# A two-block transformer kernel: order of the wide projection's chunks, and the place of the local-attention heads

## What is computed

```python
h = rms_norm(x, norm_mix[i])
u = h @ w_in[i]                                  # 1024 x 8208, row-major float32
(gq, gk, gv, g_lr, g_r, mq, mk, mv, gate_a, gate_b) = jnp.split(u, points, axis=-1)
...
o_a = rms_norm(o_a, gla_out_norm[i]).reshape(B, S, GLA_HEADS * GLA_DV) * jax.nn.silu(g_r)
y_a = o_a @ w_branch_a[i]
qh = rms_norm(mq..., moba_q_norm[i]); kh = rms_norm(mk..., moba_k_norm[i])
y_b = moba_attention(qh, kh, vh) @ w_branch_b[i]   # 8 heads; 256 tokens are one block: causal attention
y = jax.nn.sigmoid(gate_a) * y_a + jax.nn.sigmoid(gate_b) * y_b
x = x + y @ w_out[i]
```

## Time and profile before

| | |
|---|---|
| median of 3 runs | 1248.38 us (1246.42 to 1248.42) |
| profiled execution | 1250.41 us, span 1248.7 us |
| busy: PE, DVE, ACT | 1158.2 us (93%), 772.7 us (62%), 570.5 us (46%) |
| mean granted TensorE clock | 0.964 |

### The profile page before, as it was taken

How to read it: one execution, slowest core, us unless ns; L and a number is a source line. 1 busy time by engine, 2 the same in 40 slices (tenths; PEclk the granted TensorE clock), 3 DMA queues, 4 the chain that set the end, 5 groups by cost and what they waited for, 6 DMA issues and landing times.

```text
span 1248.7 us, 15377 instructions
## 1 busy us (share of the span) xinstructions
PE 1158.2 (93%) x6348; PEld 971.8 (78%) x6348; DVE 772.7 (62%) x868; ACT 570.5 (46%) x783; POOL 62.1 (5%) x118
## 2 busy tenths in 40 slices
PE   4899979899999977699999899999999899999998
PEld 2677756679998756599998687787787788997886
DVE  1586668578878739687554465435656567665444
ACT  2542327565444213354443446654665356545342
POOL 2011120000111100000000000000000000000000
PEclk8999989999999878799999989999999999999999
DMA  9956680157998844387555657878652265655550
GB/s 310 382 193 221 227 292 21 68 183 236 321 339 288 273 165 149 120 266 250 178 184 180 153 122 162 155 151 163 135 200 75 71 219 184 186 183 186 185 177 34
DMA packets 119431, 236.80 MB, mean 190 GB/s; under 512 B 5569, under 2 KB 60162, under 8 KB 119234
## 3 DMA queue, kind: packets, MB, share of 16 engines
q1 hardware_dynamic: 105458, 186.26, 49.8%
q0 software_dynamic: 13904, 49.56, 11.7%
HBM read 234.75 MB, written 1.05 MB: 189 GB/s over the span
## 4 chain that ended last, share of the span: by engine, by line
PE 82%; DVE 6%; DMA 4%; ACT 3%; issue 2%; SPq 2%; DVEq 0%; ACTq 0%
PE ps L1676 17%; PE ps L1677 16%; PE ps L1678 16%; PE ps L1715 7%; PE ps L1714 7%; PE ps L1713 7%; PE ps L1795 2%; DVE modraw L1079 2%; DMA modraw<-in_w_mod 1%; PE ps L1931 1%; PE ps L1944 1%; DMA raw<-in_w_in 1%; DMA mod<-in_w_mod 1%; ACT wH L558 1%; DVE wL L1000 1%
## 5 line engine op out<-in xcount | busy, mean ns | idle before, releaser
L1000 DVE TENSOR_TENSOR wL<-raw,wH 128x1024 fp32r<-128x1024 f32 x328 | 397.6, 1222 | 309.9 <-ACT wH L558 308.5
L558 ACT ACTIVATE wH<-raw 128x1024 fp32r<-128x1024 f32 x328 | 343.1, 1057 | 440.7 <-PE ps L1678 295.9
L1676 PE MATMUL ps<-wH,aH 128*128 128x512 f32 (+1 forms) x624 | 252.6, 405 | 17.8 <-DVE aL L1028 9.9
L1677 PE MATMUL ps<-wL,aH 128*128 128x512 f32 (+1 forms) x624 | 245.8, 394 | 0.0
L1678 PE MATMUL ps<-wH,aL 128*128 128x512 f32 (+1 forms) x624 | 245.3, 393 | 0.0
L1713 PE MATMUL ps<-aH,wH 128*128 128x256 f32 x768 | 219.0, 285 | 0.0
L1715 PE MATMUL ps<-aH,wL 128*128 128x256 f32 x768 | 217.3, 283 | 0.0
L1714 PE MATMUL ps<-aL,wH 128*128 128x256 f32 x768 | 217.3, 283 | 0.0
L1676 PEld LDWEIGHTS ps<-wH,aH 128*128 128x128 f32 x624 | 120.3, 193 | 52.6 <-issue 24.8
L1713 PEld LDWEIGHTS ps<-aH,wH 128*128 128x128 f32 x768 | 147.4, 192 | 0.7 <-issue 0.5
L1714 PEld LDWEIGHTS ps<-aL,wH 128*128 128x128 f32 x768 | 147.4, 192 | 0.7 <-issue 0.7
(11 more groups left out here) (295 smaller groups left out, 1227.2 us busy)
## 6 DMA issues: line engine op xcount, KB each, us to landing
raw<-in_ffn_w_in SPq DMA_DIRECT2D x88, 512.0 KB
modraw<-in_w_mod POOLq DMA_DIRECT2D x80, 512.0 KB, 6.1
raw<-in_w_in SPq DMA_DIRECT2D x32, 1024.0 KB
raw<-in_ffn_w_out SPq DMA_DIRECT2D x22, 1024.0 KB
raw<-in_w_up SPq DMA_DIRECT2D x16, 1024.0 KB
raw<-in_w_down SPq DMA_DIRECT2D x16, 1024.0 KB
mod<-in_w_mod SPq DMA_DIRECT2D x8, 1024.0 KB, 12.5
raw<-in_attn_w_qkv SPq DMA_DIRECT2D x8, 1024.0 KB
```

What stands on the lines that cost most here:

```text
L558: nc.scalar.activation(wH[:, n % WS, :], raw[:, (n // 2) % RAW, (n % 2) * 1024:(n % 2) * 1024 + 1024], ACT.Copy).then_inc(w_hi, 1)
L1000: V.tensor_tensor(wL[:, n % WL, :], raw[:, (n // 2) % RAW, (n % 2) * 1024:(n % 2) * 1024 + 1024], wH[:, n % WS, :].bitcast(fp32), ALU.subt ...
L1676: T.matmul(outp, xh, h, start=first, stop=False)
L1677: T.matmul(outp, xh, l, start=False, stop=False)
```

## The change

The chunks of the projection are taken in the order 0, 2, 1, 3, ... (the loads and the columns of `u` that are written). The `mqk` groups stand behind chunks 12 and 13, four groups each, in banks 4 to 7. Score products 0 and 1, the `oa` groups and `moba(0)` stand inside chunks 14 and 15, `moba(1)` behind chunk 15. `bra` runs tile 0 first, then tile 1, from tiles `oaH` and `oaL` of its own, with the remaining `moba(h)` in front of some of its parts (`hooks`: the pair is sub, tile). The splits of the `brb` weights stand between the heads.

Of the new functions, `mprobs(h)` is the copy of the transposed probabilities that stood in the loop before (it waits for `mtranspose(h)` and for `mvalues(h - 2)`); `gate_a(t)` multiplies tile t of the `bra` product with its gate; `oa_groups(i)` issues groups i and i + 1 of `oa`; `ob_first` waits for all eight `moba_out` and transposes tile 0 of the attention output, `ob_last` tile 1, into banks 6 and 7; `hi_ob` and `lo_ob` write their high and low parts.

```diff
+MQK = (0, 4, 1, 5, 2, 6, 3, 7)
+WIN = (0, 2, 1) + tuple(range(3, 16))
+...
+        def mbank(j):
+            return ps[:, 4 + j % 4, :]
@@ sync queue
-            for c in range(16):
-                chunk(n + 4 * c, a["w_in_2"][0], c * CW if c < 4 else LR0 + GRANK + (c - 4) * CW)
+            for i, c in enumerate(WIN):
+                chunk(n + 4 * i, a["w_in_2"][0], c * CW if c < 4 else LR0 + GRANK + (c - 4) * CW)
@@ ScalarE: beside(c, j), after the split of weight piece (c, j)
-                if c >= 13 and j == 0:
+                elif (c, j) in ((13, 0), (14, 0)):
                     mqk_out(c - 13)
+                elif (c, j) == (14, 3):
+                    mexp(0)
+                    mexp(1)
+                elif c == 15 and j < 2:
+                    for i in (2 * j, 2 * j + 1):
+                        hi(GROUPS["oa"] + i, oaH[:, 2 * i:2 * i + 2, :], gain=gcol[:, 24 + 2 * i:26 + 2 * i])
+                elif (c, j) == (15, 2):
+                    mprobs(0)
             def mqk_out(step):
-                for j in (2 * step, 2 * step + 1):
+                for i in range(4 * step, 4 * step + 4):
+                    j = MQK[i]
...
@@ ScalarE: behind the projection
-            mqk_out(3)
-            for j in range(4):
-                hi(GROUPS["oa"] + j, aH[:, 2 * j:2 * j + 2, :], gain=gcol[:, 24 + 2 * j:26 + 2 * j])
-            mexp(0)
-            for h in range(H):
-                adv(SUBS["bra"] + WS + h)
-                if h + 1 < H:
-                    mexp(h + 1)
+            n = SUBS["brb"]
+            for h in range(1, H):
+                if h + 1 < H:
+                    mexp(h + 1)
+                if h == H - 2:
+                    adv(n)
+                elif h == H - 1:
+                    for k in range(1, 3):
+                        adv(n + k)
+                mprobs(h)
+            for k in range(3, 5):
+                adv(n + k)
+            for j in range(2):
+                hi_ob(j)
+            for k in range(5, 8):
+                adv(n + k)
+            for j in range(2, 4):
+                hi_ob(j)
@@ VectorE: called after beside(c, j)
+            def moba_beside(c, j):
+                if c == 14 and j >= 2:
+                    mmax(j - 2)
+                elif c == 15 and j in (0, 2):
+                    for i in (j, j + 1):
+                        lo(GROUPS["oa"] + i, oaL[:, 2 * i:2 * i + 2, :], oaH[:, 2 * i:2 * i + 2, :],
+                           gain=gcol[:, 24 + 2 * i:26 + 2 * i], k_hi=hcount[0])
+                        hcount[0] += 1
+                elif (c, j) == (15, 3):
+                    mmax(2)
+                    mmax(3)
@@ VectorE: behind the projection
-            lo4("oa", aL, aH, gain=gcol[:, 24:32])
-            mmax(0)
-            mmax(1)
-            for h in range(H):
-                adv(SUBS["bra"] + WS + h)
-                if h + 2 < H:
-                    mmax(h + 2)
-                if h >= 1:
-                    moba_out(h - 1)
+            n = SUBS["brb"]
+            for h in range(2, 6):
+                moba_out(h - 2)
+                mmax(h + 2)
+            moba_out(4)
+            gate_a(0)
+            adv(n)
+            for k in range(1, 3):
+                adv(n + k)
+            moba_out(5)
+            for k in range(3, 5):
+                adv(n + k)
+            moba_out(6)
+            moba_out(7)
+            for j in range(2):
+                lo_ob(j)
+            for k in range(5, 8):
+                adv(n + k)
+            gate_a(1)
+            for j in range(2, 4):
+                lo_ob(j)
@@ TensorE: behind(c), after chunk c
-                elif c >= 12:
...
-                    for j in (2 * (c - 12), 2 * (c - 12) + 1):
-                        group(GROUPS["mqk"] + j, ...)
+                elif c in (12, 13):
...
+                    for i in range(4 * (c - 12), 4 * (c - 12) + 4):
+                        j = MQK[i]
+                        if i >= 4:
+                            pe.wait_ge(t_lo, GROUPS["mqk"] + i - 3)
+                        for m in range(4):
+                            lo_ = 3072 + (2 * j + m // 2) * P
+                            ins = T.transpose(mbank(i)[:, m * P:(m + 1) * P], u[:, m % 2, lo_:lo_ + P], ident)
+                        ins.then_inc(t_done, 1)
+                elif c == 14:
+                    pe.wait_ge(oa_ready, 1)
+                    oa_groups(0)
+                elif c == 15:
+                    moba(1)
+            def within(c, s):
+                if (c, s) == (14, 1):
+                    mscores(0)
+                    mscores(1)
+                elif (c, s) == (15, 1):
+                    oa_groups(2)
+                elif (c, s) == (15, 2):
+                    moba(0)
             def mscores(h):
-                pe.wait_ge(t_lo, GROUPS["mqk"] + 5 + h // 2)
+                pe.wait_ge(t_lo, GROUPS["mqk"] + 8)
@@ TensorE: behind the projection
-            mscores(0)
-            mscores(1)
-            pe.wait_ge(oa_ready, 1)
-            groups("oa", xn)
-            rows_mm(SUBS["bra"], UNITS["bra"], aH, aL, KT, GROUPS["oa"], moba, tiled=False)
-            mvalues(H - 1)
-            pe.wait_ge(m_oout, H)
-            tile_groups("ob", xn, 0)
+            pe.wait_ge(t_lo, GROUPS["oa"] + 4)
+            rows_mm(SUBS["bra"], UNITS["bra"], oaH, oaL, KT, None,
+                    hooks={(1, 0): lambda: moba(2), (3, 0): lambda: moba(3), (5, 0): lambda: moba(4),
+                           (7, 0): lambda: moba(5), (1, 1): lambda: moba(6), (3, 1): lambda: moba(7),
+                           (5, 1): lambda: mvalues(H - 1), (7, 1): ob_first})
             rows_mm(SUBS["brb"], UNITS["brb"], aH, aL, KT, GROUPS["ob"],
-                    hooks={(2, 0): tile_ready("ob", xn, m_oout, H), (4, 1): tile_ready("y", xn, oa_ready, 2, 0)})
+                    hooks={(2, 0): ob_last, (4, 1): tile_ready("y", xn, oa_ready, 2, 0)})
```

More of the change, by code:

```diff
@@ L142 @@
 HIDDEN = {"in0": 0, "in1": 9, "up": 18}
-TILE0 = {name: i + 1 for i, name in enumerate(("wo", "out0", "pool", "out1", "brb", "wo2", "down", "pg", "ple"))}
+WIN = (0, 2, 1) + tuple(range(3, 16))
+TILE0 = {name: i + 1 for i, name in enumerate(("wo", "out0", "pool", "out1", "bra", "brb", "wo2", "down", "pg", "ple"))}
 SUB_OF = (("q", "qkv", 4, 0), ("k", "qkv", 4, 8), ("v", "qkv", 4, 16), ("wo", "wo", 0, 4), ("in0", "in0", 4, 0),
@@ L296, in build @@
         sB.close()
+        oaH, oaL = (oa[:, j, 0:2, :].rearrange("p b (k s) -> p (b k) s", s=S) for j in range(2))
+        def mbank(j):
+            return ps[:, 4 + j % 4, :]
         gsq = st[:, 0:2, :, :].rearrange("p t h e -> p (t h) e")
@@ L820, in rms, with hi_ob @@
                     hi_t(name, j, gain=gain)
+            def hi_ob(j):
+                t, k0 = j // 2, 4 * (j % 2)
+                act.wait_ge(t_done, GROUPS["ob"] + j + 1)
+                nc.scalar.activation(aH[:, k0:k0 + 4, t * P:(t + 1) * P],
+                                     mbank(2 + j % 2).rearrange("p (k s) -> p k s", k=4), ACT.Copy).then_inc(t_hi, 1)
             act.wait_ge(lrw_in, 16)
@@ L880, in beside @@
                         .then_inc(go_sd, 1)
-                if c >= 13 and j == 0:
+                elif (c, j) in ((13, 0), (14, 0)):
                     mqk_out(c - 13)
+                elif (c, j) == (14, 3):
[6 more added lines that the diff above has]
+                    mprobs(0)
             def mqk_out(step):
-                for j in (2 * step, 2 * step + 1):
-                    g = GROUPS["mqk"] + j
-                    act.wait_ge(t_done, g + 1)
-                    nc.scalar.activation(mT[:, 2 * j:2 * j + 2, :], tbank(g).rearrange("p (h s) -> p h s", h=2), ACT.Copy,
+                for i in range(4 * step, 4 * step + 4):
+                    j = MQK[i]
+                    act.wait_ge(t_done, GROUPS["mqk"] + i + 1)
+                    nc.scalar.activation(mT[:, 2 * j:2 * j + 2, :], mbank(i).rearrange("p (h s) -> p h s", h=2), ACT.Copy,
                                          scale=gcol[:, 33:34] if j < 4 else gcol[:, 32:33]).then_inc(t_lo, 1)
[L892 to L907, removed]
-            mqk_out(3)
-            for j in range(4):
-                hi(GROUPS["oa"] + j, aH[:, 2 * j:2 * j + 2, :], gain=gcol[:, 24 + 2 * j:26 + 2 * j])
             def mexp(h):
@@ L931, in _ @@
                 nc.scalar.activation(pT[:, h % 2, :], ps[:, 4, 0:3 * P], ACT.Copy).then_inc(m_Tc, 1)
-            for j in range(4):
-                hi_t("ob", j)
+            for c in range(16):
+                for j in range(3):
+                    adv(n + 4 * c + WS + j)
+                    beside(c, j)
+                if c == 0:
+                    for t in range(TT):
+                        rms_tile(t, ln_x, 8)
+                    act.wait_ge(xn_ready, TT)
+                act.wait_ge(w_used, summed("win", c))
+                w = WIN[c]
+                for t in range(TT):
+                    ins = nc.scalar.activation(u[:, t, w * CW:(w + 1) * CW], pair(un + c)[:, t, :],
```

(32 more changed lines are left out.)

31 lines of the change are left out of this document (27 added, 4 removed).

## The result

The changed kernel takes 1257.05 us (median of 5 runs, 1256.45 to 1263.14) against 1248.38 us of the kernel before: the ratio is 1.0095 with an interval of [1.0071, 1.0119]. Forecast were 1254.3 us, +5.9, and "slower" by more than 0.2% with a chance of 0.69; the medians say +8.7 us, the ratio +8.9 to +14.9. The profiled execution has 1257.0 us and a span of 1255.3 us, 6.6 us more than before.

What follows compares the result with a forecast made beforehand. TensorE, busy 93% of the span, was taken as the bound. Order -7.4, net stops +9.9 and clock +3.4 gave +5.9 us: 1256.3 profiled, 1254.3 us median; range 1251 to 1259 alone, 1246 to 1262 with rivals 2 and 3.

Steps and rivals of the forecast that it cites:

- The stops: New TensorE waits in chunks 14, 15 and `bra`: 17.25 us, for 7.3 us of old ones that go; 9.9 us more.
- group 2 of `oa`: Inside chunk 15 after sub 1: TensorE ready at 6.4 us, group may start at 9.0; stop 2.6 us.
- copy for head 1: Inside `bra`: probabilities copy ready at 6.35 us, wanted by TensorE for `moba(2)` at 3.3; stop 3.05 us.
- The two small ones: Extra TensorE stops: 0.35 us before `oa` group 3 in chunk 15, 0.25 us for `moba_out(0)` in `bra`.
- Rival 1: The cover holds: waits met in time, 1233.7 us, chance 0.08; half-way, 8.5 us of stops, 1242.2 us, chance 0.09.
- The clock in the heads: Half-clock stretches behind the five new stops of 2.6 us or longer: two falls taken, 3.4 us more.
- The order: Start of the wide projection: loading chunk 2 second shortens TensorE's stops and keeps the full clock, 7.4 us less.
- The second stop: Start of the wide projection, TensorE's wait before 717.49 us: shrinks from 1.90 to 0.5 us, 1.4 less.
- Rival 2: The chunk order brings nothing, chunk 2 being as slow as chunk 1 there: 1261.7 us, chance 0.13.
- The sum: Whole kernel: -7.4 + 9.9 + 3.4 = +5.9 us; profiled execution 1256.3 us, median 1254.3 us.
- Rival 3: The halves cancel: no clock drops, stops a quarter less, 1246.6 us, or in full 1250.9; chance 0.13.

Runs made afterwards that it cites:

- e2: The changed kernel with the old chunk order (natural), so the heads edit alone; 1263.21 us, ratio 1.0123 to the kernel before.
- e3: The changed kernel with VectorE's low parts of `oa` groups 2 and 3 moved from behind split (15, 2) to behind (15, 1); 1252.34 us, ratio 1.0049.
- e4: The changed kernel with `moba_out(5)` before the splits of `brb` subs 1 and 2, `moba_out(6)` before 3 and 4; 1247.61 us, ratio 1.0008.
- e5: e3 with `mexp(0)`, `mexp(1)` behind the `oa` high parts in chunk 15, and `mmax(2)`, `mexp(2)` before that chunk's scaling; 1250.63 us, ratio 1.0033.
- e6: e5 with the VectorE order of e4 besides; 1240.36 us against 1246.55 for the kernel before, ratio 0.9949.
- e9: e6 with `moba_out(0)` in front of `mmax(3)`, and `mexp(0)`, `mexp(1)` both behind the last `oa` high parts; ratio 0.9970 to the kernel before.
- e10: e6 with the natural chunk order; 1244.00 us against 1244.89 for the kernel before, ratio 0.9998.
- e1: The kernel before with only the chunk order changed to 0, 2, 1, 3; 1243.61 us against 1245.42, ratio 0.9982.
- e8: The kernel before with chunk order 1, 0, 2, 3, so chunk 1 first; ratio 0.9965.
- e7: The kernel before with chunk order 0, 3, 1, 2, 4, so another odd chunk second; ratio 0.9983.

## Why the prediction was right, and where it was not

**The stops: right, each for its reason.** The largest term, 17.25 us, stood on chains worked out from rows 4, 8, 9 and 10. In the order of the prediction:

| | predicted | measured |
|---|---|---|
| `mscores(0)` | 0.75 | 0.80 |
| group 2 of `oa` | 2.6 | 2.64 |
| `mtranspose(0)` | 4.1 | 4.13 |
| copy for head 1 | 3.05 | 3.22 |
| `mvalues(6)` | 2.9 | 2.95 |
| `mvalues(7)` | 3.25 | 3.28 |

The two small ones, 0.35 us in front of group 3 and 0.25 for `moba_out(0)`, are not shown as waits. The first can be seen in e2 and e3: at the full clock the eight transposes behind the 2.65 us stop take 1.44 us, and those of groups 0 and 1 take 1.03. e3 and e4 took three of the six stops away by moving the waiting item in front of the split, without taking out work, and the others stayed as they were: for these three it is shown that they were queue order. For those of 2.64 and 3.22 us e5 shows that the order sets them, but part of the wait moved on; the one of 0.80 us was not tested. Rival 1, that the free 54 and 38% of ScalarE and VectorE would cover them, fell for the reason given: the chain starts with TensorE's own last product.

**The clock in the heads: the size of this execution was missed, and the size is not fixed.** The term was 3.4 us, for two falls of the clock at five stops. The profiled execution of the change had four, and 15.7 - 9.7 = 6.0 us; e2, with the same heads code and the same stops, had two, 3.4 us. So two was neither wrong nor shown: the number differs from one execution to the next, and the reason given for two (that part of each would fall into waits on the other engines) accounts for less than 1 us of the 6.8. A single trace, before or after, does not give this term.

**The order: right in its mechanism, and 1.4 us too high for this execution.** The product behind sub 4 was forecast at 708.4 us on the clock of before; it came at 705.73 + 3.08 = 708.8. The stop was 1.85 us and not 1.4, and "stops of 1.4 and 0.5 us should not lower the clock" did not hold for it: the stretch of 706 to 710 us stands at 0.57, which is 0.43 x 4 = 1.7 us. The second stop, given 0.5, vanished in that slower stretch. So 5.9 - 1.9 = 4.1 of stops and 3.4 - 1.7 of clock, 5.8 us by terms and 6.0 by the stretch, for 7.4 predicted. In e3, e4, e5, e6 and e9, with the same order and stops of 1.76 to 2.00 us, the clock stayed at 1.00 there and the stretch was 28.84 to 29.07 us, 7.1 to 7.3 less than before's. But before's own 3.4 us of clock were not fixed either: e2 and e10, in the natural order, lost 1.7 us there. Against these two the order gave 4.1 and 5.0 us in the start stretch, and 1.6 us of it went in the stretch behind.

Whole runs give for the order 0.18, 0.28, 0.35 and 0.49% in e1, in the change against e2, in e8, and in e6 against e10 (2.2 to 6.1 us). Rival 2, no gain from the order, is excluded by e6 against e10 and by e8; e1 alone does not do it, since e7, with an odd chunk second, shows 0.17% as well. How much of 2 to 6 us a whole run gains is not settled.

**The sum.** Predicted for one execution was +5.9 between the same places; measured +9.7: 2.6 us from the clock in the heads and 1.4 from the order, less the 0.2 us by which the stops came out below their sum. Nearly all of the 3.8 us is the clock. In whole runs the medians moved by +8.7 us (1257.05 - 1248.38), and the ratio's interval begins at +8.9, so the forecast was low by some 3 us or more there too. The profiled spans would have said +6.6, which looks nearer to the forecast only because the profiled execution of after was 3.1 us ahead before it came to the change. The executions of one kernel spread by more than that: of 25 of the kernel before beside e1 to e4, the shortest took 1240.63 us at a mean granted clock of 0.973, the longest 1253.64 us at 0.961.

**Rival 3** (the halves cancel) needed a clock that does not fall, with the stops in full or a quarter shorter; the stops came in full, and the clock fell.

## What to carry to other kernels

In an in-order queue, ask of every item that the bound engine waits for what stands in front of it, and whether that begins with the bound engine's own last product: such a wait is not covered by free time, however much there is, and moving the item one place forward (e3, e4) can remove it whole. Count a stop of 2 us or more on TensorE as itself and something for the clock: each fall costs 1.7 us, and the 23 stops over 2 us in the heads of the eight traces with the new heads went with 15 falls, about 1.1 us a stop on average. Take that term from several executions, not from one. When one wait is taken away, work out the next one behind it before counting the gain: in e5 and e9 it had been covered by the one removed.

## What the runs showed of the hardware

- The granted clock fell to about half at stops of 1.85, 2.64, 2.95, 3.28 and 4.13 us and not at one of 3.22 us (the change). With the same stops in e2 it fell at 4.13 and 2.95 us only. It did not fall at stops of 1.77 us (e8), 2.00 us (e3) and 2.39 us (e6), and did at 2.39 us in e1 (0.57 over 708 to 712 us). The length of a stop alone does not decide it here.
- Each fall cost TensorE 1.7 us, or two or three times that where falls stand in a row: 3.4 us over 938 to 946 us in e9, 5.1 us in the stretch between (3.4 us in e2, e8 and e10).
- Of `w_in` (rows 32,832 bytes apart, 2,048 bytes of each row in a chunk) chunks 0 and 2 load at 295 to 324 GB/s and chunks 1 and 3 at 146 to 181 GB/s, in first, second or third place and with the clock full or lowered; the first half of chunk 1 in e7 went at 279 GB/s. Why is not known.
